# Second block's mixer: heads in pairs, and the stick-breaking sums as two passes of rounded parts

## The reference

```python
# stick-breaking attention, 4 heads of 64
z = q @ k.T * 64 ** -0.5                  # key position < query position, else masked
log_1m_beta = -softplus(z)                # 0 where masked
tail = reverse_cumsum(log_1m_beta) - log_1m_beta     # sum over later keys
attn = exp(log_sigmoid(z) + tail)
y_sb = attn @ v
# retention, 4 heads of 64
y_ret = ((rotary(q) @ rotary(k).T) * decay) @ v      # causal; then normed and gated
# conformer convolution: 31 taps over time, and a short gated convolution
```

## Time and profile before

| | us |
|---|---|
| median of 3 runs (2907.69 to 2911.49) | 2910.93 |
| the profiled execution | 2907.59 |
| its span, first to last instruction | 2905.7 |
| TensorE matmul busy in it | 2517.2 (87%) |
| VectorE busy | 1109.9 (38%) |
| ScalarE busy | 778.1 (27%) |
| GpSimd busy | 167.2 (6%) |
| mean granted clock of TensorE | 0.945 of full speed |

### The profile page before, as it was taken

One profiled execution on the slowest core, in us unless ns is written; L12 is line 12 of the kernel. 1 busy time (PEld: TensorE's weight loads), 2 busy tenths in 40 slices (PEclk: granted clock), 3 DMA queues, 4 the chain that ended last, 5 costly groups with the idle time before them and its releaser, 6 DMA issues. The chain is left out here.

```text
span 2905.7 us, 36841 instructions
## 1 busy us (share of the span) xinstructions
PE 2517.2 (87%) x14450; PEld 1866.6 (64%) x14450; DVE 1109.9 (38%) x1689; ACT 778.1 (27%) x1311; POOL 167.2 (6%) x287
## 2 busy tenths in 40 slices
PE   8895998877498969987884598999999989999998
PEld 7574665444266655654442576788887867888887
DVE  4653010000444541000002555655652555655542
ACT  3430110000145510110000342544332342543321
POOL 0000111111000001111110000000000000000000
PEclk9997999999699979999997799999999999999999
DMA  5228999999421079999995321313333111223231
GB/s 154 56 82 344 406 406 407 409 408 406 173 87 44 8 310 407 402 407 411 407 409 231 108 70 44 116 59 101 102 116 116 66 58 46 100 88 101 88 130 51
DMA packets 174816, 576.40 MB, mean 198 GB/s; under 512 B 20496, under 2 KB 104016, under 8 KB 125042
## 3 DMA queue, kind: packets, MB, share of 16 engines
q1 hardware_dynamic: 164146, 558.07, 50.5%
q0 software_dynamic: 10560, 16.81, 1.7%
HBM read 569.56 MB, written 23.07 MB: 204 GB/s over the span
## 5 line engine op out<-in xcount | busy, mean ns | idle before, releaser
L1158 PE MATMUL ps<-first_weights,moe_xsT 128*64 128x256 f32 x2688 | 312.0, 381 | 48.9 <-DMA first_weights<-in_moe_w_up 32.2
L226 PE MATMUL ps<-l_h_hi,l_w_hi 128*128 128x512 f32 x896 | 352.9, 394 | 0.0
L228 PE MATMUL ps<-l_h_hi,l_w_lo 128*128 128x512 f32 x896 | 348.8, 389 | 0.0
L227 PE MATMUL ps<-l_h_lo,l_w_hi 128*128 128x512 f32 x896 | 348.7, 389 | 0.0
L1214 DVE TENSOR_TENSOR moe_hid<-moe_silu,ps 128x256 f32<-128x256 f32 x64 | 27.0, 421 | 795.8 <-PE ps L1158 795.8
L1158 PEld LDWEIGHTS ps<-first_weights,moe_xsT 128*64 128x64 f32 x2688 | 224.2, 137 | 146.3 <-issue 96.7
L2634 DVE TENSOR_TENSOR l_w_lo<-l_raw,l_w_hi 128x2048 fp32r<-128x2048 f32 x76 | 174.0, 2292 | 312.8 <-ACT l_w_hi L2404 312.8
L1195 ACT ACTIVATE moe_ys<-ps 128x512 f32<-128x512 f32 x64 | 38.2, 597 | 689.5 <-PE ps L1176 689.5
L1176 PE MATMUL ps<-first_weights,moe_hidT 128*64 128x512 f32 x672 | 180.6, 686 | 38.6 <-DVE moe_hidT L1216 38.6
L1158 PE MATMUL ps<-first_ring,moe_xsT 128*64 128x256 f32 x1408 | 167.5, 387 | 32.5 <-DMA first_ring<-in_moe_w_up 18.2
L2404 ACT ACTIVATE l_w_hi<-l_raw 128x2048 fp32r<-128x2048 f32 x76 | 145.1, 1912 | 174.4 <-PE ps L228 163.5
(11 more groups left out here) (549 smaller groups left out, 4355.4 us busy)
## 6 DMA issues: line engine op xcount, KB each, us to landing
first_weights<-in_moe_w_up SPq DMA_DIRECT2D x84, 1024.0 KB, 29.0
first_weights<-in_moe_w_down SPq DMA_DIRECT2D x84, 1024.0 KB, 28.8
first_weights<-in_moe_w_gate SPq DMA_DIRECT2D x84, 1024.0 KB, 28.5
first_ring<-in_moe_w_gate SPq DMA_DIRECT2D x44, 1024.0 KB, 28.1
first_ring<-in_moe_w_up SPq DMA_DIRECT2D x44, 1024.0 KB, 28.9
first_ring<-in_moe_w_down SPq DMA_DIRECT2D x44, 1024.0 KB, 29.0
l_raw<-in_ffn_up SPq DMA_DIRECT2D x44, 1024.0 KB, 5.1
l_raw<-in_w_in SPq DMA_DIRECT2D x24, 1024.0 KB, 5.2
```

Of the source, the lines that this page charges most:

```text
L226: pe.matmul(out, stationary[0], moving[0], start=first, stop=False)
L227: pe.matmul(out, stationary[0], moving[1], start=False, stop=False)
L228: return pe.matmul(out, stationary[1], moving[0], start=False, stop=last)
L1158: ins = pe.matmul(k.ps[64 * h:64 * h + 64, 2 + m, 0:256], xsT[:, j, :], weights.gate_up[s][m][:, j, 256 * h:256 * h + 256], start=j == 0, ...
```

## The change

1. **Pairs.** Scores and retention scores are made for two heads at once: head 2p from rows 0 to 63, head 2p + 1 from rows 64 to 127, in two different PSUM banks, with only 64 rows in use in each product. The zeroed halves and the memsets go. The mix of two heads is interleaved too, into output partitions 0 to 63 and 64 to 127 of one bank.
2. **Chunks.** The key tiles go in three chunks, (0), (1) and (2, 3), of 512, 384 and 384 columns. The first two are made by `sb_first` or `ret_first`, the third by `sb_last` or `ret_last`, at another place in TensorE's list, since it takes the banks of the first again.
3. **Rounded parts.** softplus (now in `ln1[hd % 2]`) is rounded to fp32r by ScalarE (`high_of_sp`), the rest is formed by VectorE (`low_of_sp`), and `tri` multiplies both parts in fp32r by an fp32r copy of the constants (`exact`): twenty products for ten.
4. **Whole heads.** ScalarE's Exp, Ln, weights and VectorE's addition take 1280 columns at a time.
5. **Order.** All three lists are rewritten. `spin` uses bank 7.

```diff
+                def pair_scores(tile, c, keys, queries, masked, made):
+                    for kt in CHUNKS[c]:
+                        at = TRI_AT[kt] - TRI_AT[CHUNKS[c][0]]
+                        banks = [k.ps[:, 2 + 2 * (c % 2) + half, :] for half in range(2)]
+                        for half in range(2):
+                            rows_of = slice(64 * half, 64 * half + 64)
+                            ins = pe.matmul(banks[half][:, at:at + wide(kt)], keys[rows_of, tile, kt * P:(kt + 1) * P], queries[rows_of, tile, kt * P:],
+                                            start=True, stop=not masked)
...
+                        if masked:
+                            for half in range(2):
+                                ins = pe.matmul(banks[half][:, at:at + P], k.identb[:, :], k.masksb[:, :], start=False, stop=True)
...
+                def sb_last(p):
+                    pe.wait_ge(x.z_kept, 6 * p + 2)
+                    pair_scores(p, 2, sbk, sbq, True, x.scored)
+                def tri(hd):
+                    pe.wait_ge(x.sp_low, hd + 1)
+                    for c in range(3):
+                        if hd % 2 and c:
+                            pe.wait_ge(x.subbed, 3 * (hd - 1) + c)
+                        at = TRI_AT[CHUNKS[c][0]]
+                        for kt in CHUNKS[c]:
+                            o = TRI_AT[kt] - at
+                            for kk in range(kt, NT):
+                                lead = (kk - kt) * P
+                                for part in (sp_hi, sp_lo[hd % 2]):
+                                    ins = pe.matmul(k.ps[:, TRI_BANKS[hd % 2][c], o + lead:o + wide(kt)], exact[:, int(kk > kt), :],
...
+                def pair_mix(p, bank, src, v_at, out):
                     for kt in range(NT):
+                        for half in range(2):
+                            hd, o = 2 * p + half, 64 * half
+                            ins = pe.matmul(k.ps[o:o + 64, bank, kt * P:SEQ], vt[:, v_at, kt, hd * HD:(hd + 1) * HD], src[half][:, TRI_AT[kt]:TRI_AT[kt] + wide(kt)],
...
+                def ret_mix(p):
+                    pe.wait_ge(x.ret_done, 8 * p + 8)
...
+                def high_of_sp(hd):                                   # ScalarE
+                    act.wait_ge(x.sp_done, hd + 1)
+                    if hd:
+                        act.wait_ge(x.tri_made, 3 * hd)
+                    act.activation(sp_hi[:, :], ln1[hd % 2][:, :], ACT.Copy).then_inc(x.sp_high, 1)
...
+                def low_of_sp(hd):                                    # VectorE
+                    dve.wait_ge(x.sp_high, hd + 1)
+                    dve.tensor_tensor(sp_lo[hd % 2][:, :], ln1[hd % 2][:, :], sp_hi[:, :].bitcast(F32), ALU.subtract).then_inc(x.sp_low, 1)
```

More of the change, by code:

```diff
@@ L2159, in tri @@
[L2159 to L2175, removed]
+                def pair_scores(tile, c, keys, queries, masked, made):
[6 more added lines that the diff above has]
+                                            start=True, stop=not masked)
+                            if not masked:
+                                ins.then_inc(made, 1)
+                        if masked:
+                            for half in range(2):
+                                ins = pe.matmul(banks[half][:, at:at + P], k.identb[:, :], k.masksb[:, :], start=False, stop=True)
+                                if kt == CHUNKS[c][-1]:
+                                    ins.then_inc(made, 1)
@@ L2189, in ret_scores, with ret_first @@
-                def ret_scores(hd):
-                    tile, half = hd // 2, hd % 2
-                    if hd == 0:
+                    pe.matmul(k.ps[:, 7, :], k.const(C_RR), src, start=True, stop=True).then_inc(x.spun, 1)
+                def ret_first(p):
+                    if p == 0:
                         pe.wait_ge(x.placed, 4)
[L2193 to L2198, removed]
@@ L2202, in ret_mix @@
                         pe.wait_ge(x.ro_kept, 1)
-                    mix(hd, 7, wr, 1, x.ret_done, x.ret_mixed)
-                for u in range(4, 8):
+                    pair_mix(p, 7, wr[2 * p:2 * p + 2], 1, x.ret_mixed)
+                for u in range(4, 9):
                     project(u)
-                project(8)
-                pe.wait_ge(x.zeroed, 6)
-                scores(0)
+                sb_first(0)
                 project(9)
                 project(10)
+                sb_last(0)
@@ L2224, in mixer @@
-                spin(0)
                 spin(1)
+                sb_last(1)
+                project(16)
+                project(17)
+                spin(2)
+                project(18)
                 tri(2)
-                scores(3)
-                project(16)
-                pe.wait_ge(x.kept, DONE[RK])
-                spin(2)
+                project(19)
                 spin(3)
-                project(17)
-                sb_mix(2)
-                project(18)
-                project(19)
@@ L2695, in decayed @@
[L2695 to L2700 removed]
+                    dve.wait_ge(x.ln_done, hd + 1)
+                    dve.scalar_tensor_tensor(ln1[hd % 2][:, :], z[hd % 2][:, :], 0.0, ln1[hd % 2][:, :], ALU.max, ALU.add).then_inc(x.sp_done, 1)
@@ new lines, in decayed @@
+                def decayed(p, c):
+                    if p and c == 0:
+                        dve.wait_ge(x.sb_mixed, 2)
+                    for kt in CHUNKS[c]:
+                        at = TRI_AT[kt] - TRI_AT[CHUNKS[c][0]]
+                        for half in range(2):
+                            dve.wait_ge(x.ret_made, 8 * p + 2 * CHUNKS[c][-1] + half + 1)
+                            dve.tensor_tensor(wr[2 * p + half][:, TRI_AT[kt]:TRI_AT[kt] + wide(kt)], k.ps[:, 2 + 2 * (c % 2) + half, at:at + wide(kt)],
+                                              decay[:, 2 * p + half, 0:wide(kt)], ALU.mult).then_inc(x.ret_done, 1)
@@ L2728, in mixer @@
                 softplus(0)
+                softplus(1)
+                low_of_sp(0)
+                low(l, 6)
                 taps(2)
-                low(l, 6)
                 subtract(0)
-                softplus(1)
+                low_of_sp(1)
                 taps(8)
@@ L2735, in mixer @@
                 subtract(1)
-                softplus(2)
-                taps(4)
-                low(l, 8)
                 dve.wait_ge(x.tables_in, 16)
```

256 lines of the change are left out of this document (127 added, 129 removed).

## The result

The changed kernel takes 2879.98 us, the median of 4 runs (2878.04 to 2882.22), against 2911.21 for the kernel before (4 runs beside it): a ratio of 0.990 with an interval of 0.988 to 0.991, faster by 31 us. The profiled execution took 2882.22 us.

A forecast was written before the change was run, and what follows sets the result against it. TensorE was taken to bound the mixers. Per layer -23.5 own work, -13.1 old waits, +17.2 new waits, +6.6 low clock make -12.8; 25 us kept over two layers, 2910.9 to 2886, range 2870 to 2903.

The forecast's parts named there:

- A: TensorE's stop ahead of tri(0): low_of_sp(0) stands behind softplus(1) on VectorE; 12.9 us chain, wait 4.6 us.
- B: TensorE's stop ahead of tri(2): the same chain with high 8 and a kept unit, 14.9 us; wait 5.4 us.
- C: TensorE's stop ahead of ret_mix(1): decayed(1, 2) stands behind low 11 on VectorE; 5.7 us with no cover.
- low clock behind A, B, C: Slow TensorE clock after each of the three stops: 2.2 us each, 6.6 us per layer.
- TensorE's own work: Pairs of scores and retention scores, mixes in pairs and fp32r sums take 23.5 us less per layer on TensorE.
- rival 3: Each change between 64-row and 128-row products costs 0.16 us, 16 more changes per layer, 2.6 us: 2891; chance 0.06.
- The waits that come: New TensorE stops in the mixer, A, B, C and two smaller ones: 17.2 us per layer.
- old waits: Stops that go: 8.8 us for l_rq, 2.3 of slow clock behind it, two of some 1.0; 13.1 per layer.
- Rival 1: The clock stays up through A, B and C: 13 us less, 2873; chance 0.17.
- Rival 5: Low clock lasts through the work after A, B and C: 20 us a layer more, 2927, slower; chance 0.05.
- Rival 2: In the sums, fp32r products of 128 columns are as slow as f32: 6.6 us in all, 2893; chance 0.12.
- Rival 4: Halves don't overlap in pairs and mixes, two heads cost two: 16 us per layer more, 2918; chance 0.04.

The follow-up runs named there:

- all three exchanges: Changed kernel with VectorE's low_of_sp(0) ahead of softplus(1), low_of_sp(2) ahead of softplus(3), and decayed(1, 2) ahead of low 11: 2850.91 us, 0.980 of the kernel before.

## Why the prediction was right

The forecast was 2886, with 2870 to 2903 and 0.88 on faster; 2880 came. Its net per layer was 12.8 us; the mixers gave 12.6 and 13.6. Term by term, in layer 0:

| | forecast | measured |
|---|---|---|
| two heads' scores with masks | 3.0 | 3.59 (2.22 + 1.37) |
| two heads' retention scores | 2.55 | 2.56 |
| two heads' mix | 2.30 | 2.30 |
| one head's sums, full clock | 2.74 | 2.8 |
| A, B, C | 4.6, 5.4, 5.7 | 4.12, 4.90, 5.38 |
| ahead of `spin(0)`, `ret_last(1)` | 0.9, 0.6 | 0.7, 0.3 |
| low clock behind A, B, C, next unit counted in | 6.6 | 7.0 (2.9 + 2.5 + 1.6); layer 1: 5.3 |

- **TensorE's own work** was right but for one term. The scores cost 0.6 a pair more, 1.2 a layer, and the sums 0.3. The step that failed is the one that weighed the Trainium skill's rule on tiling modes: I read from the earlier trace rows that there is no drain, since the 64-row, 32-row and full products follow each other without a visible gap. A cost of this kind does not show as a gap: it lies in the spacing. The 0.96 and 0.745 a pair that I took from those rows are themselves 0.1 above the 0.85 and 0.64 of their columns: one way out of the 64-row products, 0.21, spread over two pairs. In the changed kernel every pair of the scores pays it whole. Two experiments put a change at about 0.16 us in the mean, the price rival 3 named, though not 16 of them a layer: a pair's scores pay for about four, the retention scores and the mixes for none that the sum had not in it already.
- **The waits that come** were named rightly, with their engines, places and causes, and each was 0.2 to 0.5 too long, 1.8 in all. This is the larger half of what made the forecast right: own work and old waits alone would have given 36.6 a layer. The errors have opposite signs and leave the sum where it was, and that it came out within 0.2 us in layer 0 is luck. Layer 0: -22.1 of own work at full clock (forecast 23.5), -12.9 of waits gone (8.8 and 1.9 idle, 2.2 of clock), +15.4, +7.0 make -12.6. Layer 1: -22.1, -12.2, +15.4, +5.3 make -13.6.
- **The clock.** Rival 1 (it stays up) is out for the changed kernel: the granted clock is 0.50, 0.50 and 0.58 behind waits of 4.12, 4.90 and 5.38 us, 0.50 being 1.2 GHz of 2.4. The 2.2 us for each place is near the mean (2.3 and 1.8) and not right for one place: the same 4.12 us ahead of `tri(0)` cost 2.9 in layer 0 and 1.6 in layer 1. And the rival did come about once, in layer 1 of the run with the scores in turn, where the granted clock stayed up behind 3.60 us of idle time and the sums took 2.8 (shown there). Rival 5 (it stays low) is out too: from 1764.07 on, half a microsecond behind the sums, the next unit runs at its usual 0.12 a product. It decided from 12.8 us a layer, and the low clock cost 7.0 and 5.3.
- **Rival 2** is out by the run with f32 sums and by the 0.06 and 0.11 in the timeline. The estimate was 0.11 for each. The product of the high part takes 0.06 and that of the low part 0.11, but the product behind the two takes 0.05 longer than its columns (384 columns 0.23 at 1724.25, 0.17 at 1724.48), so two of them come to 0.22 after all, and a head's sums to 2.8. The estimate was right; of its reason, that 128 columns of weights were never loaded anew faster than in 0.12, the mask products at 0.06 in the earlier trace rows already showed the contrary for bf16.
- **Rival 4** (no overlap) is out by the mix at 2.30 and the run with it in turn.
- **The 6 us between 2886 and 2880** are not the change's as far as the traces tell: the spans moved by 25.3, where the sum had 25. For the rest there is the scatter of the first block, which is larger than this.
- What the prediction did not ask is whether its waits were bound to come. It laid the lists beside each other as they are; the experiments show that three exchanges of neighbours in VectorE's list, each found by asking what stood in front of the late operation, are worth as much as the change.

## What to carry to other kernels

When a change takes work off the bounding engine, lay out what the other engines' lists then do to it: here 35 us of relief a layer (36.6 by the forecast) turned into 13, and the missing part could be named beforehand. In an in-order list an operation that is ready must not stand behind one that isn't; look at the idle time in brackets ahead of the instruction in front of the late one, and exchange the two. Before writing a large change, try the small edit that takes away the largest single wait alone.

## What the runs showed of the hardware

- A change between f32 products on 64 rows and full products costs about 0.16 us of TensorE's time in the mean (0.31 for two, 1.09 for seven), some 0.21 out of the 64-row products and 0.10 back, and a single product on 64 rows of 512 columns holds off a full one for 1.06 us, as long as a pair does.
- The time that a wait costs on top of itself, since the granted clock stands at 0.50 in the work behind it, is not fixed by its length. The 4.12 us ahead of `tri(0)` cost 1.5 to 2.9 us more in ten cases with it, the 5.38 ahead of the last mix 1.4 to 2.9 in twelve, and 3.60 us cost 2.7 in one layer and nothing in the other. Behind waits of up to 1.7 us (all three exchanges) the granted clock was 1.00 throughout, in both mixers. A comparison of single executions can be off by 2 to 3 us by this alone.
- Two f32 products into different halves of the output partitions overlap almost wholly when issued by turns (2.30 for twice 1280 columns), and in part (3.86) when one head's come first: the second head's records then start 1.56 us behind the first's.
- fp32r products of 128 columns follow each other at 0.06 and 0.11 us by turns, less than the 0.12 of 256 columns, and the product behind such a two takes 0.05 longer than its columns.
